# A two-block transformer kernel: the first block's early modulation made in two column halves

## The reference

```python
c_act = jax.nn.silu(c)
mod = c_act @ w_ada[l] + b_ada[l]                        # 1 x 6144
sh1, sc1, gt1, sh2, sc2, gt2 = jnp.split(mod, 6, axis=-1)
u = _rmsnorm(h, g_mix[l]) * (1 + sc1[:, None, :]) + sh1[:, None, :]
proj = u @ w_in                                          # q, k, v, us, g_att, g_ssm
```

## Time and profile before

| | us |
|---|---|
| median of 3 runs (lowest, highest) | 2054.67 (2052.28, 2055.97) |
| the profiled execution | 2055.66 |
| its span | 2053.9 |
| PE busy in the span | 2024.5 |
| DVE, ACT, POOL busy | 1081.5, 647.7, 1299.3 |

### The profile page before, as it was taken

How to read it: one execution, slowest core, us unless ns; L and a number is a source line. 1 busy time by engine, 2 the same in 40 slices (tenths; PEclk the granted TensorE clock), 3 DMA queues, 4 the chain that set the end, 5 groups by cost and what they waited for, 6 DMA issues and landing times. The chain is left out here.

```text
span 2053.9 us, 25791 instructions
## 1 busy us (share of the span) xinstructions
PE 2024.5 (99%) x10047; PEld 1682.4 (82%) x10047; DVE 1081.5 (53%) x1387; ACT 647.7 (32%) x1070; POOL 1299.3 (63%) x757
## 2 busy tenths in 40 slices
PE   6999999999999999999999999999999999999998
PEld 3888888888888877788888888888787888888888
DVE  6971255455463585665532377632554555634554
ACT  3202233233331364444400035433434433221103
POOL 2537544665255539998844555876787888858650
PEclk8999999999999999999999999999999999999999
DMA  9545545454454214323475240333133322188432
GB/s 372 132 101 155 170 138 173 145 154 138 154 179 144 105 40 144 103 89 137 147 282 206 74 163 22 123 118 129 62 123 123 123 103 83 52 332 312 144 134 82
DMA packets 185192, 293.24 MB, mean 143 GB/s; under 512 B 12824, under 2 KB 136688, under 8 KB 184048
## 3 DMA queue, kind: packets, MB, share of 16 engines
q1 hardware_dynamic: 175088, 268.53, 39.1%
q10 hardware_dynamic: 9984, 23.07, 3.0%
HBM read 211.64 MB, written 79.94 MB: 142 GB/s over the span
## 5 line engine op out<-in xcount | busy, mean ns | idle before, releaser
L954 POOL TENSOR_SCALAR w_h<-raw 128x512 fp32r<-128x512 f32 (+2 forms) x110 | 241.9, 2199 | 370.7 <-issue 146.3
L1471 PE MATMUL ps<-tb,w_h 128*128 128x512 f32 x1344 | 420.6, 394 | 2.9 <-DVE quads L2708 2.4
L1034 POOL TENSOR_TENSOR w_l<-raw,w_h 128x512 fp32r<-128x512 f32 x210 | 302.9, 1450 | 109.3 <-ACT w_h L2020 109.1
L1471 PEld LDWEIGHTS ps<-tb,w_h 128*128 128x128 f32 x1344 | 251.5, 188 | 63.6 <-DVE quads L2708 4.2
L1471 PE MATMUL ps<-tb,w_l 128*128 128x512 f32 x672 | 264.6, 394 | 0.0
L956 POOL TENSOR_TENSOR w_l<-raw,w_h 128x512 fp32r<-128x512 f32 (+2 forms) x110 | 205.6, 1869 | 9.2
L2020 ACT ACTIVATE w_h<-raw 128x512 fp32r<-128x512 f32 x210 | 131.0, 628 | 254.7 <-PE ps L1471 168.2
L1471 PE MATMUL ps<-act_h,w_h 128*128 128x512 f32 x504 | 197.0, 391 | 0.3 <-ACT quads L2049 0.2
L1471 PE MATMUL ps<-act_l,w_h 128*128 128x512 f32 x504 | 196.9, 391 | 0.0
L1471 PE MATMUL ps<-act_h,w_l 128*128 128x512 f32 x504 | 196.0, 389 | 0.0
L1471 PEld LDWEIGHTS ps<-tb,w_l 128*128 128x128 f32 x672 | 126.2, 188 | 28.2
(11 more groups left out here) (414 smaller groups left out, 4558.6 us busy)
## 6 DMA issues: line engine op xcount, KB each, us to landing
raw<-in_w_in SPq DMA_DIRECT2D x45, 1024.0 KB, 5.5
raw<-in_w_up SPq DMA_DIRECT2D x16, 1024.0 KB, 5.4
f_scratch<-r SPq DMA_DIRECT2D x16, 1024.0 KB, 7.9
gates_scratch<-quads SPq DMA_DIRECT2D x24, 512.0 KB, 7.4
r<-gates_scratch SPq DMA_DIRECT2D x12, 1024.0 KB, 8.1
ada_lo<-in_w_ada SPq DMA_DIRECT2D x16, 512.0 KB, 3.8
ada_hi<-in_w_ada SPq DMA_DIRECT2D x16, 512.0 KB, 4.7
gates_scratch<-gate_st ACTq DMA_DIRECT2D x32, 256.0 KB, 2.1
```

The costliest lines, as they stand in the source:

```text
L954: nc.gpsimd.tensor_scalar(w_h[:, k, c, :], src[:, c, :], 1.0, None, ALU.mult).then_inc(s["w_high"], 1)
L1034: nc.gpsimd.tensor_tensor(w7_l[:, SLOTS[o]], x, w7_h[:, SLOTS[o]].bitcast(F32), ALU.subtract)\
L1471: last = nc.tensor.matmul(bank_of(n, bank), w[:, SLOTS[o], c, :], x(c), start=(first and c == 0 and p == 0), stop=(c == KD // 2 - 1 and p ...
```

## The change

The early modulation is cut in two halves by columns instead of a cut by rows and by engine. Half 0 holds shift and scale of channels 0 to 511, half 1 those of channels 512 to 1023. PE multiplies the shift columns (one matmul of 512 columns for each chunk of rows), DVE multiplies and adds up the scale columns (128x512), and PE adds DVE's sum as a second row.

```diff
-SUMMED = 1
-ADA_PARTS = ((0, 2), (2, 4), (4, 6), (6, 7), (7, 8))
-ADA_PE = 10
+SUMMED = 2
+ADA_PARTS = ((0, 0, 4), (0, 4, 8), (1, 0, 1), (1, 1, 4), (1, 4, 8))
...
-            single(0)
+            pool.wait_ge(s["g_row_in"], 16)
+            split_half(0, 0, 1, s["w_half"])
+            pool.wait_ge(w_in_[0], 16)
+            split_half(0, 1, 2, s["w_split"])
+            pool.sem_inc(s["passed"], 1)
...
+            def ada_rows(i):
+
+                h, lo, hi = ADA_PARTS[i]
+                pe.wait_ge(ada0_in[i], 32)
+                for c in range(lo, hi):
+                    nc.tensor.matmul(ada_dst[h], c_one[:, c, 0, :], ada_shift[h][:, c, :],
+                                     start=(c == 0), stop=False, skip_group_check=True)
...
+            ada_rows(0)
+            ada_rows(1)
             for t in range(QB):
+                if t == 2:
+                    ada_scales(0, s["colt"])
+                    ada_columns(0)
+                    pe.wait_ge(s["colt_read"], 1)
+                    pe.wait_ge(s["mod_read"], 1)
                 pe.wait_ge(x_in[t // 2], 16)
...
+            product_pair((0, 1), 0, KD, act_h, act_l, s["u_ready"], split=0, head=s["head0"],
+                         within={(1, 0): lambda: ada_rows(3), (2, 0): second_half_rows, (2, 2): lambda: ada_columns(1)})
...
+            scaled(0, h1)
+            head_low()
+            scaled(1)
+            low(0, h1)
+            dve.wait_ge(s["head0"], 3)
+            scaled(2)
+            ada_early(3)
+            low(1)
+            scaled(3)
+            ada_early(4)
+            low(2)
+            low(3)
+            turns_and_rest()
+            modulation_half(1)
+            dve.wait_ge(s["mod_ready"], 2)
+            scaled(4)
+            scaled(5)
+            for c in range(4, KD):
+                low(c)
+                if c + 2 < KD:
+                    scaled(c + 2)
```

More of the change, by code:

```diff
@@ L497, in _, with ada_part_in, first, first_half_of @@
             sp.dma_start(c_row[:], a["c"].flatten().rearrange("(r p) -> r p", p=P)).then_inc(c_in, 16)
+            def ada_part_in(i):
+                h, lo, hi = ADA_PARTS[i]
+                for m, w in enumerate((ada_shift, ada_scale)):
+                    col = slice(m * D + h * HALF, m * D + h * HALF + HALF)
+                    sp.dma_start(w[h][:, lo:hi, :], weights("w_ada", col, row=lo * P, k=hi - lo)).then_inc(ada0_in[i], 16)
+            def first(k, col):
+                sp.dma_start(raw[:, k, :, :], weights("w_in", bass.ds(col, NB))).then_inc(w_in_[k], 16)
+            def first_half_of(half, done):
+                lo = half * KD // 2
+                sp.dma_start(raw[:, 0, lo:lo + KD // 2, :],
+                             weights("w_in", bass.ds(3 * ATT, NB), row=lo * P, k=KD // 2)).then_inc(done, 16)
+            ada_part_in(0)
+            ada_part_in(1)
             for t in range(0, QB, 2):
@@ L500, in _ @@
                   .then_inc(x_in[t // 2], 16)
[L501 to L513, removed]
-            def first(k, col):
-                sp.dma_start(raw[:, k, :, :], weights("w_in", bass.ds(col, NB))).then_inc(w_in_[k], 16)
[L518 to L522, removed]
+            first_half_of(0, s["g_row_in"])
+            ada_part_in(2)
+            ada_part_in(3)
+            first_half_of(1, w_in_[0])
+            ada_part_in(4)
             first(1, 0)
@@ L1273, in ada @@
                 return last
-            ada_dst = ps[0:4, 0, 0:HALF]
+            ada_dst = ps[0:4, 3, HALF:T], ps[0:4, 2, 0:HALF]
             def ada_rows(i):
[L1279 to L1283, removed]
@@ L1294, in _, with second_half_rows @@
             spread.then_inc(s["rstd_ready"], 1)
[L1295 to L1302, removed]
-                last = nc.tensor.transpose(slot(2)[:, 4 * j:4 * j + 4], ada_line[:, P * j:P * j + P], ident[0:4, 0:4])
-            last.then_inc(s["ada_done"], 1)
-            product_pair((0, 1), 0, KD, act_h, act_l, s["u_ready"], split=0, head=s["head0"])
+            def second_half_rows():
+                ada_rows(4)
+                ada_scales(1, s["tr"])
+            product_pair((0, 1), 0, KD, act_h, act_l, s["u_ready"], split=0, head=s["head0"],
+                         within={(1, 0): lambda: ada_rows(3), (2, 0): second_half_rows, (2, 2): lambda: ada_columns(1)})
             pe.wait_ge(s["s5_in"], 16 * 7)
```

218 lines of the change are left out of this document (128 added, 90 removed).

## The result

The changed kernel takes 2058.78 us in the median (2054.69 to 2060.54), against 2054.13 (2051.59 to 2055.97) for the kernel before, measured beside it: a ratio of 1.0023, with a 95% interval from 1.0015 to 1.0032. It is slower by 3.1 to 6.6 us. The forecast was 2057.7, inside its range of 2051 to 2063. The profiled execution took 2060.54 with a span of 2058.8.

The account below looks back on a forecast made before the run. TensorE, busy 2024.5 of 2053.9 us, was taken as the bound, with the end of `act_l` of chunk 6 deciding; -10.6 + 10.9 + 1.5 + 1.2 = +3.0 us gave 2057.7, range 2051 to 2063.

Parts of the forecast that it names:

- What counts: Behind the normalization: the end of `act_l` of chunk 6, 66.05 us before, sets the time through GpSimd's split, not the projection's start.
- The first `nrm`: At the start: first normalization step at 36.2 us instead of 46.76, bounds 33.9 to 38.
- the term of -10.6: At the start: the head start in us that the earlier first `nrm` was to give.
- The price of the vectors: In the loads: small vectors coming beside the large loads add 1.0 us, so half 0 is complete at 16.
- The normalization: From first `nrm` to `act_l` of chunk 6: 30.2 us instead of 19.3, a cost of 10.9.
- (a): TensorE's half clock at half 1's three matmuls and part of chunk 1: taken 1.5 us, bounds 0 and 5.
- (b): GpSimd's `w_l` holding VectorE's diagonal or first `act_l`: taken 1.2 us, bounds 0 and 3.7.
- rival 1: Clock stays at half after chunk 0, through half 1's three matmuls and chunk 1: 5 us instead of 1.5, 2061.2; chance 0.27.
- After the projection: 17 short VectorE operations move behind the normalization, 3.4 us; 2 of 5.5 us cover before `krylov` left; taken 0.
- The sum: Whole kernel: -10.6 + 10.9 + 1.5 + 1.2 = +3.0 us, giving 2057.7 in the median.
- the prediction's own bound: Whole kernel: below 2050.6 us faster (0.08), above 2058.8 slower (0.42), between them same (0.50).

Follow-up runs that it names:

- e4: The changed kernel with GpSimd beginning the second projection's split at 6 finished chunks instead of 7; 2055.92 us.
- e8: The edits of e3, e4, e6 and e7 together on the changed kernel, with no new edit; 2052.82 us.
- e6: The changed kernel with TensorE transposing the small vectors behind its matmuls of the first part of half 0, not ahead of them; 2060.53 us.
- e9: e8 plus three unused matmuls before the last x tiles, angles split over two waits, projection weights' second half loaded ahead of w_ada's part 3; 2049.26 us.
- e5: The changed kernel with eight short matmuls of no use filling TensorE's gaps to keep the clock up; 2056.30 us.
- e1: The changed kernel without TensorE's seven products of chunks 1 to 7 of half 1, so its shift is wrong; 2055.00 us.
- e3: The changed kernel with half 1's products moved: three chunks behind the spread, four between projection chunks 0 and 1, the sum ahead of chunk 2; 2054.14 us.
- e7: e3 with VectorE computing the angles while it waits for the spread, not ahead of the second `mod`; 2053.26 us.
- e10: e3 with the second half of the projection's weights loaded ahead of part 3 of w_ada; 2053.35 us.
- e2: The changed kernel with all of half 1, on TensorE and VectorE, ahead of the projection again; 2056.45 us.

## Why the prediction was right, and where it was not

**What counts.** It said that the end of `act_l` of chunk 6 carries the time, through GpSimd's chain. That end moved by 5.86 us, TensorE's step on `w_l` by 5.71 and `krylov` by 5.70. This held. In e4, where GpSimd's chain began one chunk sooner, TensorE's wait on `w_l` was gone and `krylov` came 1.9 us sooner behind the start of the second projection.

**The first `nrm`** was put at 36.2 and came at 39.76: the term of -10.6 was -7.0. Two steps of the working failed. The price of the vectors was added to the loads (1.0 us on half 0's landing), but TensorE waits for the vectors in front of half 0: 12.30 instead of 10. With that the six copies end at 34.95 instead of 32.4. And the spread was costed at 1.98, full clock; it took 3.27. How large the first error is, one execution can't say: in the eight kernels that wait for the vectors in this way the copies end at 32.86 to 34.95, in part since the eight products of half 0 take 8.29 to 9.84 us, so against the 32.5 of e8 it is 0.4 to 2.5 us. The profiled execution of the change lies at the bad end of it, and was the slowest of its ten.

The rest of the path was sized well. In e6, e8 and e9, where half 0 begins at about 10, its matmuls are done at 19.9, 19.8 and 19.7 (19.9 predicted); in e8 and e9 the copies are done at 32.5 and 32.6 (32.4); in e9, with the clock up, the first `nrm` comes at 36.31 (36.2). The weights release GpSimd at 28.39 and 35.31 in the change (28 and 35.5 predicted). e6 mended the vectors alone and gained nothing, since the clock then fell in more places; e5 mended the clock alone, and the spread came back to 1.99.

**The normalization** was put at 30.2 and, with (a) 1.5 and (b) 1.2, at 32.9; it took 71.9 - 39.76 = 32.15. Its mechanism, seven products and the sum of TensorE ahead of VectorE's second `mod`, is shown by e1 and e3: with the products left out 3.2 of the 4.65 us are back, with the products moved 4.1. In the traces, from the first projection matmul to `act_l` of chunk 6, it is 3.7 and 5.2 us.

**(a) The clock** was right in kind and near in size: the three chunks of half 1 took 4.43 us, 1.7 more than the 2.74 of the same matmuls at full clock in e5. Chunk 1 behind them ran at full clock, so of rival 1's 5 us a third came. What the term lacked is the spread.

**(b) GpSimd** cost nothing on the path here, since the first `nrm` was so late that `act_l` at 41.36 came just as `w_l` ended (39.03 + 2.35). In e1, e3, e5, e8 and e9, with an earlier `nrm`, the hold came, 1.2 to 1.7 us each, and 0.6 in e6, within the bounds. The rule from the Trainium skill that the prediction drew on ("SBUF — State Buffer", "Who interferes with whom") agrees with the rows of e7 and e10: with two SBUF inputs 0.24 became 2.40 us beside a `w_l` begun 0.03 us sooner, and `act_l` took 0.75 with `w_l` over.

**After the projection** it said that 2 us of cover are left ahead of `krylov`. VectorE was done at 102.16 (the last row of `krylov`, 100.93 and 1.23) and TensorE came at 102.75: 0.6 left, since GpSimd held four of the moved steps. Taken as 0 for the time, rightly.

**The sum** said +3.0; `act_l` of chunk 6 shows +5.86. The term of the start was 3.6 too good, (b) was 1.2 too dear, and normalization and clock together cost 0.5 more than said. The profile after was to show VectorE waiting some 3 us and `act_l` of chunk 6 ending near 69; VectorE waited 5.13, and `act_l` ended at 71.9. By the sum alone the forecast would be 2.9 too low. It was 1.1 too low (2057.7 against 2058.78), because the medians differ by 4.65 only and because it started from a median 0.5 higher than that of the longer series (2054.67 against 2054.13). So the sign and the mechanism were right, and part of the nearness was luck. By the prediction's own bound (slower above 2058.8) the result lies on the edge between its "same" and its "slower".

## What to carry to other kernels

When work is split so that a stage can start sooner, the second part is still due: ask in which wait of its engine it lies, not only whether it fits between other work. Here the same seven products cost 4 to 5 us ahead of the projection's chunks 1 and 2, and nothing that the times show with three behind the spread and four directly behind chunk 0. And where several hindrances lie in a row (late vectors, the fallen clock, GpSimd's hold, the next split), mending one may show nothing until the others are gone too: e6 alone gained nothing, e9, which mends several, 3.8 us against the kernel before (2.1 to 5.7).

## What the runs showed of the hardware

- The same four matmuls of the spread took 1.98, 1.99, 2.74, 3.20, 3.27, 3.27, 3.40, 3.68 and 3.78 us in kernels without a filler (e1, e2, e3, e7, the change, e4, e6, e8, e10), always behind 2.4 to 2.6 us of standing still between x's transposes and the matmuls ahead of the spread. With three short matmuls in that wait they took 1.99 and 1.98 (e5, e9): two of two at full clock, against two of nine. Why e1 and e2 kept the clock without them stays open, and each figure is of one execution.
- The 16 small DMAs of vectors are issued by one engine in a row. ScalarE spends 0.3 to 0.7 us on each and issues the last at 6.7 to 7.3 us; TensorE is released by it 4.9 to 5.1 us later, at 11.6 to 12.3. The first 2 MB of w_ada, issued by SyncE at 1.7 and 2.1 us, were there at 9.9 to 10.2 (e6, e8, e9). More than half of the time until the vectors are there is thus the time until the last is issued. Whether they would land sooner if they were issued sooner, or from two queues, no run tests.
- Where a GpSimd step that reads SBUF and a VectorE step with two SBUF inputs overlapped at the start, the one that began later took longer than alone. GpSimd's `w_h` (one SBUF input) took 2.77 with VectorE standing still (e3), but 3.64, 3.53 and 3.74 where VectorE's diagonal (two SBUF inputs) had begun 0.2 to 0.3 us before it (the change, e7, e9). In e10 `w_h` began first: it took 2.77, and the diagonal 1.79 instead of 1.23. VectorE's first `nrm`, with one input in SBUF and one in PSUM, took its usual 0.75 beside `w_l` in the change.
